# A depthwise convolution shared by three engines: ScalarE makes every product of GpSimd's chunk, and GpSimd takes 10 taps instead of 6 of the last two chunks

## The reference

```
def _conv_mixer(h, w_in, dw, db, ln_g, ln_b, w_out):
    a, b, g = jnp.split(h @ w_in, 3, axis=-1)
    y = a * jax.nn.sigmoid(b)
    y = lax.conv_general_dilated(
        y, dw[:, None, :].astype(y.dtype), window_strides=(1,),
        padding=[(CONV_WIDTH // 2, CONV_WIDTH // 2)],
        dimension_numbers=('NWC', 'WIO', 'NWC'),
        feature_group_count=BRANCH) + db
    y = jax.nn.silu(_layernorm(y, ln_g, ln_b)) * jax.nn.silu(g)
    return y @ w_out
```

## Time and profile before

| | |
|---|---|
| median of 3 runs | 1827.03 us (1825.49 to 1828.29) |
| the profiled execution | 1832.89 us, its span 1830.8 us |
| PE busy | 1736.8 us (95% of the span) |
| DVE busy | 935.4 us (51%) |
| ACT busy | 593.3 us (32%) |
| POOL busy | 754.3 us (41%) |
| mean granted clock of PE | 0.966 of full speed |
| chain that ended last, by engine | issue 61%, POOL 25%, PE 2%; POOL w_lo L428 24%, POOL cv_y L498 1% |

### The profile page before, as it was taken

The page is one execution under the profiler, slowest core; times in us unless marked ns, Lnnn a source line. Parts: engine busy times, 40 slices in busy tenths (PEclk is TensorE's granted clock), DMA queues, the critical chain, the costliest instruction groups (busy, mean ns, idle before and its releaser), DMA issues.

```text
span 1830.8 us, 22444 instructions
## 1 busy us (share of the span) xinstructions
PE 1736.8 (95%) x7730; PEld 1391.9 (76%) x7730; DVE 935.4 (51%) x1213; ACT 593.3 (32%) x817; POOL 754.3 (41%) x349
## 2 busy tenths in 40 slices
PE   6999899969899999999999899999999899999997
PEld 3677577757767788888887788878877688888886
DVE  1789878866747755555557527163363611111114
ACT  3324453223323332222233333233333342222223
POOL 0599713344305344444444423433333243444442
PEclk8999899989999999999999999999999899999998
DMA  8344524434316355455453222312222122322321
GB/s 327 138 175 162 196 83 150 161 109 179 127 46 207 116 184 193 178 185 198 175 179 130 92 68 81 102 61 98 69 75 66 55 92 92 104 92 84 112 83 55
DMA packets 64718, 232.35 MB, mean 127 GB/s; under 512 B 7184, under 2 KB 7184, under 8 KB 64400
## 3 DMA queue, kind: packets, MB, share of 16 engines
q1 hardware_dynamic: 64656, 231.50, 36.2%
HBM read 229.38 MB, written 2.10 MB: 126 GB/s over the span
## 4 chain that ended last, share of the span: by engine, by line
issue 61%; POOL 25%; PE 2%; POOLq 1%; ACT 0%; DVE 0%; DVEq 0%
POOL w_lo L428 24%; POOL cv_y L498 1%; PE bank L1245 1%; PE bank L1246 1%; PE bank L1247 1%; POOLq L427 0%; POOLq L501 0%; ACT x L843 0%; POOL cv_y L491 0%; DVE m_buf L904 0%; PE ps_bc L1351 0%; PE ps_stat L1333 0%; PE ps_mrow L1327 0%; DVE x L944 0%; ACT sq L540 0%
## 5 line engine op out<-in xcount | busy, mean ns | idle before, releaser
L428 POOL TENSOR_TENSOR w_lo<-w_raw,w_hi 128x1024 fp32r<-128x1024 f32 x272 | 670.0, 2467 | 1031.8 <-ACT w_hi L516 988.9
L1245 PE MATMUL bank<-h_hi,w_hi 128*128 128x512 f32 x1344 | 531.6, 396 | 12.1 <-POOL w_lo L428 7.1
L1247 PE MATMUL bank<-h_hi,w_lo 128*128 128x512 f32 x1344 | 525.9, 391 | 0.0
L1246 PE MATMUL bank<-h_lo,w_hi 128*128 128x512 f32 x1344 | 525.8, 391 | 0.0
L516 ACT ACTIVATE w_hi<-w_raw 128x1024 fp32r<-128x1024 f32 x268 | 281.4, 1052 | 266.9 <-PE bank L1247 255.9
L1245 PEld LDWEIGHTS bank<-h_hi,w_hi 128*128 128x128 f32 x1344 | 254.1, 189 | 76.3 <-DVE h_lo L908 9.9
L1247 PEld LDWEIGHTS bank<-h_hi,w_lo 128*128 128x128 f32 x1344 | 253.8, 189 | 53.9
L1246 PEld LDWEIGHTS bank<-h_lo,w_hi 128*128 128x128 f32 x1344 | 253.8, 189 | 52.9 <-issue 1.1
L1245 PE MATMUL bank<-f_hi,w_hi 128*128 128x512 f32 x624 | 245.3, 393 | 7.4 <-DVE f_lo L936 4.4
L1247 PE MATMUL bank<-f_hi,w_lo 128*128 128x512 f32 x624 | 243.4, 390 | 0.0
L1246 PE MATMUL bank<-f_lo,w_hi 128*128 128x512 f32 x624 | 243.3, 390 | 0.0
(11 more groups left out here) (160 smaller groups left out, 1620.8 us busy)
## 6 DMA issues: line engine op xcount, KB each, us to landing
mods_ring<-w_mods_in SPq DMA_DIRECT2D x148, 512.0 KB, 5.3
w_raw<-ff_in_in SPq DMA_DIRECT2D x88, 512.0 KB, 3.5
w_raw<-ret_in SPq DMA_DIRECT2D x64, 512.0 KB, 3.4
w_raw<-ff_out_in SPq DMA_DIRECT2D x32, 512.0 KB, 3.4
w_raw<-cv_ab_in SPq DMA_DIRECT2D x16, 512.0 KB, 7.8
w_raw<-ff_tail_in SPq DMA_DIRECT2D x16, 384.0 KB, 3.1
cv_acc<-w_mods_in SPq DMA_DIRECT2D x8, 512.0 KB, 8.4
w_raw<-cv_g_in SPq DMA_DIRECT2D x8, 512.0 KB, 7.4
```

Source lines behind the costliest of these rows:

```text
L428: pool.tensor_tensor(w_lo[:, s, :], w_raw[:, s, :], w_hi[:, s, :].bitcast(F32), ALU.subtract).then_inc(lo_done, 1)
L1245: pe.matmul(out, w_h, m_h, start=start, stop=False)
L1246: pe.matmul(out, w_h, m_l, start=False, stop=False)
L1247: return pe.matmul(out, w_l, m_h, start=False, stop=stop)
```

## The change

`ACT_TAPS` goes. ScalarE makes all 30 products of chunk 1: 18 of them (`EARLY_TAPS` is 19) in iterations 1 to 3 of the `cv_ab` loop, three behind the refill of each pair of a and b, and two each behind the silu of gate units 1 to 6. GpSimd only adds: three taps behind each y product instead of two. `POOL_TAPS` is 10 instead of 6, so VectorE has 21 taps instead of 25 of chunks 6 and 7, and GpSimd and ScalarE nine adds and nine products for each, not five.

```
-POOL_TAPS = 6
-ACT_TAPS = 13
+POOL_TAPS = 10
+EARLY_TAPS = 19
...
                     if i:
-                        for m in range(2):
-                            tap(k + 2 * q + m)
+                        for m in range(3):
+                            tap(k + 3 * q + m)
                 lo_part(SLOTS * i + 7, 3)
...
                 product = (sq, diag)[(k - 1) % 2]
-                if k < ACT_TAPS:
-                    pool.wait_ge(pool_tap, k)
-                    pool.tensor_scalar(product[:], cv_y[:, ROW + k:ROW + k + T],
-                                       vec[:, V_DW + DC * k + 1:V_DW + DC * k + 2], None,
-                                       ALU.mult).then_inc(product_ready, 1)
                 pool.wait_ge(product_ready, k)
-                if k >= ACT_TAPS:
-                    pool.wait_ge(pool_tap, k)
+                pool.wait_ge(pool_tap, k)
                 pool.tensor_tensor(cv_acc[:, 1, :], cv_acc[:, 1, :], product[:], ALU.add).then_inc(pool_tap, 1)
...
             for i in range(1, 4):
-                y_and_lo_parts(i, 4 * i - 3)
+                y_and_lo_parts(i, 6 * i - 5)
...
                 for m in range(4):
-                    tap(ACT_TAPS + 4 * q + m)
-            for k in range(ACT_TAPS + 8, TAPS):
+                    tap(EARLY_TAPS + 4 * q + m)
+            for k in range(EARLY_TAPS + 8, TAPS):
                 tap(k)
...
+            def early_products(i, q):
+
+                for m in range(3):
+                    if q or m:
+                        act.wait_ge(pool_tap, 6 * i + (3 * q + m - 6))
+                    else:
+                        act.wait_ge(pool_tap, 6 * i - 5)
+                    k = 6 * i + (3 * q + m - 5)
+                    act.activation((sq, diag)[(3 * q + m) % 2][:], cv_y[:, bass.ds(k + ROW, T)], ACT.Copy,
+                                   scale=vec[:, bass.ds(DC * k + (V_DW + 1), 1)]).then_inc(product_ready, 1)
...
                     refill("cv_ab", 2 * q + 1, i)
+                    if not isinstance(i, int):
+                        early_products(i, q)
...
                 if j < SLOTS:
                     refill("cv_g", j)
-                else:
-                    products(ACT_TAPS + 2 * j, 2)
-                if j == 1:
-                    products(ACT_TAPS, 4)
-                if j == 3:
-                    products(ACT_TAPS + 4, 4)
+                if 1 <= j <= (TAPS - EARLY_TAPS) // 2:
+                    products(EARLY_TAPS + 2 * (j - 1), 2)
                 if j % SLOTS == SLOTS - 1:
                     mods(g)
                     g += 1
-            products(TAPS - 2, 2)
             mods(g)
             products(1, POOL_TAPS - 1, 6)
```

More of the change, by code:

```diff
@@ L623, in products @@
                     act.wait_ge(pool_tap, sums_before(c, m))
-                    if (c, m) == (1, ACT_TAPS):
-                        act.wait_ge(product_ready, ACT_TAPS - 1)
                     act.activation((sq, diag)[product_of(c, m) % 2][:], cv_y[:, c * ROW + m:c * ROW + m + T], ACT.Copy,
```

## The result

The changed kernel takes **1839.7 us** (median of 4 runs, 1839.49 to 1841.01) where the kernel before takes 1826.88 (4 runs, 1825.49 to 1828.29): a ratio of **1.0072, 95% interval 1.0054 to 1.0089**. The forecast was 1831.1, its range ended at 1834.5. The sign was right, the size was not: +12.8 us for +4.1.

A forecast was written before the change was run, and what follows sets the result against it. The prediction took PE, waiting for ScalarE's mrow copy before the mean over channels, to bound the convolution's end. Its terms, 0 + 0 + 0 + 3.8 + 0.3 + 0 = +4.1 us on 1827.03, gave 1831.1 us, range 1827.5 to 1834.5.

The forecast's parts named there:

- What bounds the kernel: End of the convolution: PE is late, not the taps, because its mcol waits for ScalarE's mrow copy behind chunk 6's products.
- Part 1: cv_ab loop: chunk 1's products on ScalarE are hidden, cost 0; VectorE's second group starts at 100.5 and ends 1.85 us earlier.
- Parts 2 and 3: Chunks 6 and 7: VectorE's taps end at 210.3, worth nothing; GpSimd idles 7 us, starting chunk 6's adds about 204.2.
- Part 4: Before the mean: nine products, not five, precede the mrow copy, delaying it, mcol and the mean by 3.8 us.
- Part 5: Mean to first square: GpSimd's and ScalarE's chains arrive just covered, 0.3 us taken; w_lo parts move to 229.7, costing nothing.
- one sign that the prediction had named as wrong: At the mean's end: VectorE's centring right behind its own last add would mean that GpSimd bounds.
- The clock: TensorE in the mean: same mixture of half and full clock as before, 0; later half-clock stretch could give back some time.
- the first rival: Mean: after longer PE idle time all twelve keep_busy records run at half clock, +6.0 us, 1833.0 us; chance 0.14.
- From the profile to the median: Whole kernel: the profiled execution lies 5.9 us above the median before, and that difference is carried over to the forecast.
- GpSimd sets the end: End of the convolution: GpSimd's last add moves from 219.95 to 229.4, +9.5 us, 1836.5 us; chance 0.07.
- the clock gives the time back: Mean: clock already up at its start, twelve records save 3.1 of 3.8 us, +0.7, 1827.7 us; chance 0.15.
- VectorE's taps set nothing: Judges the rival that VectorE's taps set the convolution's end: 7.1 us off VectorE, 1819.9 us; chance 0.05.

The follow-up runs named there:

- experiment 3: Changed kernel with the mods copies (and so the mrow copy) put back behind five products of chunk 6, the other four after them: 1841.06 us, 1.0055.
- Experiment 1: Changed kernel with POOL_TAPS put back from 10 to 6, early products still on ScalarE: 1829.68 us, 0.9998 of the kernel before.
- experiment 6: Changed kernel run again: 1839.35 us, 1.0053; beside it, with only 8 of 1024 columns of the first four w_lo parts made: 1833.26 us, 1.0011.
- experiment 4: Changed kernel, but GpSimd starts the four w_lo parts only after VectorE's four pair sums (L997): 1840.79 us, 1.0056.
- experiment 7: Kernel before, but GpSimd starts the four w_lo parts only when the mean is done: 1832.58 us, 1.0011.

## Why the prediction was right in sign and wrong in size

**What bounds the kernel: right.** PE was late there, through the `mrow` copy behind ScalarE's products. GpSimd's chain, with VectorE's last add behind it, was priced as the next one, and experiment 3 shows that it is.

**Part 1 (0 us): right.** Experiment 1 measures 0.9998. VectorE's second group started at 100.81 for 100.5.

**Parts 2 and 3: right.** VectorE's taps ended at 210.7 for 210.3 and its next add waited 6.55 us; GpSimd idled 7.26 us before its first add of chunk 6, at 204.58 for 204.2.

**Part 4 (+3.8): right up to the mean.** The copy came at 215.04 for 214.7, the `mcol` at 215.68 for 215.3. The mean ended at 231.77 for 232.3, near, but by another sum: its first twelve records took 1.45 us less, and then PE waited for chunk 7.

**Part 5 (0.3, of which ScalarE's table load within 0.1 us): right as far as the first square**, which came at 233.34 for 233.1, with GpSimd's last add at 228.70 to 229.79 for 229.4. PE did wait 0.31 us for chunk 7, so GpSimd's chain and PE's met within half a microsecond. With the `mrow` copy back in its place, as in experiment 3, the stage was no faster.

The nearness has luck in it, and one sign that the prediction had named as wrong did appear. It expected VectorE to wait about 1.5 us for PE after its last add. Instead L991 came right behind the bias add, which a w_lo part held to about 232.1, 0.3 us behind the mean's end. Then ScalarE, which the prediction had covered by 0.1 us, came last: its table load and dummy run to 233.44, and the first square follows them with no wait.

**Part 5, the w_lo parts: the step that failed.** "The four w_lo parts behind it move from 219.9 to 229.7 and end near 239; PE's first matmul with them moves from 247.33 to about 251." Both times of GpSimd came true (229.75, 239.51). They were costed at nothing, because PE takes the parts up only at 247. I asked who waits for the moved work, and not what it runs beside. At its old place VectorE was idle for 6.23 us, which I had in front of me in the earlier trace rows, and read only as slack. The stretched bias add stood just ahead of that idle time (1.64 us for 128 x 8), and I passed over it. At the new place VectorE adds pairs of SBUF tiles. The price, from the table above: 2.1 us by the first `ps_stat`, 3.6 more through the half clock by the projection, 5.7 in the profile; 6.1 in the medians of experiment 6.

The Trainium skill has this rule ("SBUF — State Buffer", Who interferes with whom): a VectorE instruction with two SBUF inputs contends with a GpSimd instruction that reads SBUF, and the one that issues later waits for the whole of the other. The trace agrees: 2.77 us for 0.69, with a w_lo part begun 0.1 us before, while L991, one of whose inputs is in PSUM, kept its 0.63 us each beside the same parts (1.27 for two at 237.21). The same section of the Trainium skill has it that a `tensor_scalar` can take the shared ports too; experiment 4 shows 7.91 us for 0.87. The forecast had cited no page on this.

**The clock (0): right for the mean, wrong behind it.** The twelve records took 6.92 us, 1.45 less than the 8.37 of the earlier trace rows, though PE had idled 4.94 us for 0.71. So the first rival (+6.0), that the longer idle time puts all twelve at half clock, is not borne out by the mean. The layer norm does lose by the clock, with 3.00 us of idle time and then 16.6 us at half clock, up from 0.20 and 6.8. The rule that the prediction quoted from the Trainium skill ("TensorE: Matmul & The Clock Gate", What's actually happening) stood for that rival. The trace bears it out in part only: the clock is at 0.50 behind the 3.00 us of idle time, but stays there while PE is busy for all of the 16.6 us, and ahead of the mean it was at 1.00 from 211 to 213 us with PE idle. The bound on the later stretch "can give back at most half of its length" looked at a gain only; that it could grow, from 6.8 to 16.6 us, stood nowhere.

**From the profile to the median: wrong too.** "So I carry the difference over" took it that both profiled executions lie 5.9 us above their medians. The changed kernel's lies 1.3 above (1841.01, 1839.7). So of the 8.6 us between 1831.1 and 1839.7, 4.0 are the stage (8.1 for 4.1) and 4.6 are this. Either slip alone would have been enough: 1827.03 + 8.1 = 1835.1, and 1831.1 + 4.6 = 1835.7, both lie above the 1834.5 where the range ended. The second may in part lie in the few runs of the kernel before, three for the forecast and four for the result. Its median over 19 to 25 runs on three chips was 1828.47 to 1831.05, and executions on one chip range over 7.4 us (1826.58 to 1833.99). The changed kernel's four range over 2.4 (1838.71 to 1841.11). Where both ran on one chip, with 25 runs of the kernel before, the change cost 8.3 us, as in the profiles.

Experiment 1's profile suggests a further reason. There the granted clock was at 1.00 from 211 us on, PE took up its `mcol` at 211.04, and the mean's twelve records took 3 us less than in the earlier trace rows. In the changed kernel the clock was at 1.00 from 211 to 213 too, but PE waited for `mrow` until 215.68 and found it at 0.50. So the late copy may cost the changed kernel the short executions that the kernel before has. But no other profile with that mean, neither of the seven with ten taps (6.87 to 8.24 us for the twelve records) nor of the three others (7.97 to 8.37), shows it, and none of a short execution of the kernel before was taken. This stays open.

**The rivals.** "GpSimd sets the end" (+9.5, chance 0.07) came out nearest in size, mostly by another way: GpSimd's lateness entered through the additions that its w_lo parts held up, and only 0.31 us through PE waiting for chunk 7. Of the 3.1 us of "the clock gives the time back", 1.45 came in the mean and more than that was lost again behind it. VectorE's taps set nothing.

## What to carry to other kernels

When work off the critical path moves, look at which instructions it will run beside at its new place, not only at who waits for its result. Here GpSimd's subtractions of two SBUF tiles cost nothing while VectorE was idle or ran L991, which has one input in PSUM. They held up VectorE's additions of two SBUF tiles by 0.2 to 2.2 us each, and its four small `tensor_scalar` for nearly a whole subtraction each (7.91 us for 0.87). And a stall of 2 us in a chain of short steps can be worth more than twice that (2.1 us became 5.7 in the profile), when the granted clock falls behind it and the steps that follow are bound by PE.

## What the runs showed of the hardware that I had not expected

- The four small VectorE instructions of experiment 4 (L888, 128x128, 0.22 us each) were let through one by one between w_lo parts: 7.91 us, steps of 2.30, more than the large pair sums lost.
- The hold-up works both ways: four w_lo parts take 9.28 us with VectorE idle beside them but for the bias add, 9.76 beside two held-up sums, and 10.67 beside four (experiment 7).
- GpSimd's add of the same shape takes 1.27 us for chunk 6 and 1.09 for chunk 7, in both kernels, with VectorE busy or idle. I didn't try why.
- The clock didn't simply stay down longer after the longer idle time. In the changed kernel it averages 0.80 over the 4.9 us in which PE waits for `mrow` (210.7 to 215.6), is at 0.50 again when PE resumes, and at 1.00 from about 220.6, 3.2 us into the mean; in the kernel before it is at 0.50 all through and comes back at 219.2, 6 us into it.
